# DeltaNet preparation: the block inverse transposed by VectorE in blocks of 32x32, in place of TensorE's products with a unit matrix and ScalarE's copies

## The reference, cut to what matters

```
lower = where(strict, einsum('bhnid,bhnjd->bhnij', k_beta, k) * decay, 0.0)
rhs   = concatenate([v * beta[..., None], k_beta * exp(gc)[..., None]], axis=-1)
sol   = triangular_solve(eye(C) + lower, rhs, left_side=True, lower=True, unit_diagonal=True)
u, w  = sol[..., :dv], sol[..., dv:]
```

## Time and profile before

| | |
|---|---|
| median of 3 runs | 3337.93 us (3333.68 to 3339.06) |
| the profiled execution | 3340.42 us, its span 3338.6 us |
| PE busy over the span | 3035.5 us (91%), 24428 matmul instructions |
| DVE, ACT, POOL busy | 1317.9 us (39%), 1020.9 us (31%), 479.6 us (14%) |
| the preparation, layer 0 | from about 520 to 704 us of the span |
| the preparation, layer 1 | from about 2240 to 2426 us |
| L1372, the turns on PE | 93.3 us busy, 2880 instructions |
| L1214, the turns' copies on ACT | 57.5 us busy, 120 instructions |

### The profile page before, as it was taken

How to read it: one execution, slowest core, us unless ns; L and a number is a source line. 1 busy time by engine, 2 the same in 40 slices (tenths; PEclk the granted TensorE clock), 3 DMA queues, 4 the chain that set the end, 5 groups by cost and what they waited for, 6 DMA issues and landing times. The chain is left out here.

```text
span 3338.6 us, 64798 instructions
## 1 busy us (share of the span) xinstructions
PE 3035.5 (91%) x24428; PEld 1647.8 (49%) x24429; DVE 1317.9 (39%) x2704; ACT 1020.9 (31%) x1799; POOL 479.6 (14%) x534
## 2 busy tenths in 40 slices
PE   6998898979989999999987898989989899988996
PEld 3554676974543333433332554768955333333331
DVE  3433643444533333333326443634445333322234
ACT  2222442322223333333324232442222222222232
POOL 0010004321010000000007010005231100000004
PEclk8998998999999999999999999989989999999998
DMA  9302330013339999899859210410034599999956
GB/s 382 120 8 82 128 123 5 4 68 134 158 132 346 358 356 358 329 390 387 352 223 349 88 41 22 160 42 4 4 144 170 230 407 424 424 424 423 424 216 239
DMA packets 133673, 724.22 MB, mean 217 GB/s; under 512 B 24800, under 2 KB 42720, under 8 KB 96736
## 3 DMA queue, kind: packets, MB, share of 16 engines
q1 hardware_dynamic: 84800, 544.14, 41.8%
q0 software_dynamic: 28224, 102.77, 8.0%
q10 hardware_dynamic: 20448, 74.46, 5.5%
HBM read 619.62 MB, written 101.71 MB: 216 GB/s over the span
## 5 line engine op out<-in xcount | busy, mean ns | idle before, releaser
L2303 PE MATMUL psum<-arena 128*64 x1792 | 822.9, 614 | 61.3 <-DVE arena L2402 61.3
L2305 PE MATMUL psum<-arena 128*64 128x512 f32 x1792 | 824.5, 613 | 0.0
L2303 PEld LDWEIGHTS psum<-arena 128*64 128x64 f32 x1792 | 243.0, 141 | 542.0 <-issue 542.0
L2325 PE MATMUL psum<-arena 128*64 x896 | 408.3, 599 | 10.9 <-DVE arena L2406 10.9
L827 PE MATMUL psum<-arena 128*128 128x480 f32 (+3 forms) x1088 | 403.2, 527 | 15.7 <-PEq L164 8.4
L2327 PE MATMUL psum<-arena 128*64 128x512 f32 x896 | 408.4, 598 | 0.0
L827 PEld LDWEIGHTS psum<-arena 128*128 128x128 f32 x1088 | 207.9, 194 | 189.7 <-issue 177.8
L2273 POOL DMA_INDIRECT arena<-h,arena x112 | 109.4, 977 | 1263.1 <-PE psum L2293 1239.5
L2325 PEld LDWEIGHTS psum<-arena 128*64 128x64 f32 x896 | 123.9, 139 | 257.3 <-issue 257.3
L2410 DVE TENSOR_TENSOR arena<-arena,psum 128x256 f32<-128x256 f32 x112 | 47.2, 422 | 513.9 <-ACT arena L2359 513.8
L2371 ACT COPY arena<-arena 128x2048 f32 x114 | 217.1, 1904 | 91.6 <-DMA arena<-in_w_gu 87.6
(11 more groups left out here) (357 smaller groups left out, 4308.4 us busy)
## 6 DMA issues: line engine op xcount, KB each, us to landing
arena<-in_w_gu SPq DMA_DIRECT2D x130, 2048.0 KB
arena<-in_w_dn SPq DMA_DIRECT2D x130, 1024.0 KB
y_slots<-arena ACTq DMA_DIRECT2D x122, 512.0 KB
arena<-in_ada SPq DMA_DIRECT2D x24, 2048.0 KB
y_slots<-arena SPq DMA_DIRECT2D x4, 4096.0 KB
arena<-in_w_gdn SPq DMA_DIRECT2D x6, 1536.0 KB
arena<-in_w_out SPq DMA_DIRECT2D x2, 4096.0 KB
arena<-in_w_tok SPq DMA_DIRECT2D x4, 1920.0 KB
```

Source lines behind the costliest of these rows:

```text
L2303: nc.tensor.matmul(psum[half(0), 2 + r, :], xT[:, r, rows_of(k, 0)], W[:, bass.ds(at + k * 2 * DE, 2 * DE)], start=(k == 0), stop=(k == DK ...
L2305: last = nc.tensor.matmul(psum[half(1), 2 + r, :], xT[:, r, rows_of(k, 1)], late_gu[:, k * 2 * DE:(k + 1) * 2 * DE], start=(k == 0), stop= ...
L2325: nc.tensor.matmul(psum[half(0), bank, :], hT[r][:, rows_of(j, 0)], W[:, bass.ds(at + GU + c, 512)], start=(j == 0), stop=(j == 1))
```

## The change

The turn is done by DVE: right behind its subtraction of a level it transposes `DT` into `U`, with one instruction for 128x384 that transposes each block of 32x32 in place. Up to level 4 the blocks of the inverse are at most 32 wide, so all that lies outside the diagonal blocks of 32x32 is zero, and the result is the same. PE's `turn_inverse` and ACT's `take_inverse` are gone with the semaphore between them. The turn behind level 0 becomes `first_inverse` on DVE, behind the updates of slot 2. Two waits that the removed code had are put elsewhere: `lower` of level 1 waits for the copy of u that empties its bank, and `solve` waits for the copies of the tile before.

```
@@ scalar @@
-                        def take_inverse(G, v):
-                            for d in range(2):
-                                c = chain(G, d)
-                                act.wait_ge(tr_done[c], nth(G, v) + 1)
-                                nc.scalar.copy(U[:, G, d], psum[:, 4 + c, 0:GW]).then_inc(d_done[c], 1)
...
@@ tensor, in lower @@
                                 pe.wait_ge(d_done[c], nth(G, v - 1) + 1)
+                                if v == 1 and G >= 2:
+                                    pe.wait_ge(u_copied, 2 * (G - 2) + d + 1)
...
-                        def turn_inverse(G, v):
...
-                                        last = nc.tensor.matmul(psum[half(r), 4 + c, b], DT[half(r), G % 3, d, b], cst("unit")[half(r)], start=True, stop=True)
-                                last.then_inc(tr_done[c], 1)
...
                         def solve(G):
                             pe.wait_ge(it_done, 2 * min(G + 3, NT))
+                            if G:
+                                pe.wait_ge(wt_copied, 2 * G)
...
@@ vector @@
+                        def turn_inverse(G, d):
+                            nc.vector.transpose(U[:, G, d], DT[:, G % 3, d]).then_inc(d_done[chain(G, d)], 1)
+
+                        def first_inverse(G):
+                            for d in range(2):
+                                dve.wait_ge(dt1_done, 2 * G + d + 1)
+                                turn_inverse(G, d)
+
                         def update(G, v):
                             for d in range(2):
...
                                 nc.vector.tensor_tensor(DT[:, G % 3, d], DT[:, G % 3, d], psum[:, 4 + c, 0:GW], ALU.subtract).then_inc(dt_done[c], 1)
+                                if v < LAST:
+                                    dve.wait_ge(dt_done[c], nth(G, v - 1) + 1)
+                                    turn_inverse(G, d)
...
                             for T, v in live:
-                                if v == 1:
-                                    dve.wait_ge(dt1_done, 2 * T + 2)
                                 update(T, v)
+                            if a == 2 and G + 1 < NT:
+                                first_inverse(G + 1)
```

More of the change, by code:

```diff
@@ L1164, in phase_gdn_prepare @@
                     S("masked"), S("dt1_done"), S("u_prod"), S("wt_prod"), S("u_copied"), S("wt_copied"))
-                x_prod, x_done, dt_prod, dt_done, tr_done, d_done = [
-                    [S(f"{name}{c}") for c in range(4)] for name in ("x_prod", "x_done", "dt_prod", "dt_done", "tr_done", "d_done")]
+                x_prod, x_done, dt_prod, dt_done, d_done = [
+                    [S(f"{name}{c}") for c in range(4)] for name in ("x_prod", "x_done", "dt_prod", "dt_done", "d_done")]
                 half = lambda r: slice(64 * r, 64 * r + 64)
@@ L1226, in _ @@
                         take_q(0)
-                        take_inverse(0, 0)
                         for G, a, live in slots:
@@ L1233, in _ @@
                                 tail(G - 1)
[L1234 to L1238, removed]
                     @block.gpsimd
@@ L1396, in _ @@
                         turn_q(0)
-                        turn_inverse(0, 0)
                         for G, a, live in slots:
@@ L1411, in _ @@
                                 turn_q(G + 1)
[L1412 to L1416, removed]
                     @block.vector
@@ L1455, in update @@
                                 nc.vector.tensor_tensor(DT[:, G % 3, d], DT[:, G % 3, d], psum[:, 4 + c, 0:GW], ALU.subtract).then_inc(dt_done[c], 1)
+                                if v < LAST:
+                                    dve.wait_ge(dt_done[c], nth(G, v - 1) + 1)
+                                    turn_inverse(G, d)
                         gated(0)
+                        first_inverse(0)
                         for G, a, live in slots:
```

## The result

The changed kernel takes 3274.09 us (median of 4 runs, 3271.93 to 3276.72), the kernel before 3336.1 us (4 runs, 3333.68 to 3339.06): a ratio of 0.9814, interval 0.9802 to 0.9826. Forecast were 3270 us and a range of 3258 to 3311. The profiled executions took 3340.42 and 3274.05 us, 66.4 apart, where the sum said 67.6.

The account below looks back on a forecast made before the run. PE bounds the kernel. Per layer, first tile 4.5, four full tiles 25.9, last tile 2.4 and last levels 0.95 us sum to 33.8, so 67.6 for both: 3270 us from the median, range 3258 to 3311.

Parts of the forecast that it names:

- the sum: Whole program: savings of 33.8 us a layer in the preparation stage, 67.6 us for both layers.
- PE bounds the tile, and 7.24 us come off: Full tile: PE busy for all 27.94 us, so removing the turns leaves 20.70 us if PE never waits.
- The transpose costs 0.56 us: Each 128x384 transpose on DVE, taken from a 558 ns DVE operation of same shape in SBUF only.
- Both bounds, 0.36 and 0.96: Transpose time in us: 0.36 from below, as a copy; 0.96 from above, if a column costs twice.
- Pairs of 1.07 us, DVE's cadence of 0.47: DVE in a full tile: update plus its transpose takes 0.60 + 0.47 us; one update starts every 0.47 us.
- PE waits 0.76 us in slot 1, so 21.46 a tile: Slot 1's lower groups wait 0.02 + 0.37 + 0.37 us for late DVE; full tile 20.70 + 0.76, 6.48 less.
- The cover by `gate_rows`: Start of a tile: first transposes run under PE's gate_rows and cost nothing; uncovered, in the last tile, up to 2.3 us.
- The single loop: One level of a chain with only one tile live: period 3.74 us in place of 4.64.
- The clock: Rival: PE's granted clock stays low through the tiles after its waits; 3306 us, slower if all groups double; chance 0.03.
- quick: Rival: a transpose takes 0.36 us, as a copy, so PE never waits; 38 us a layer, 3262 us; chance 0.10.
- slow: Rival: a transpose takes 0.96 us and DVE bounds; tile 24.5 us, 15.7 a layer, 3307 us; chance 0.13.
- nothing was given back behind the barrier: Rival denied here: the stage shrinks but a later one gives it back, 3338 us; chance 0.03.

Follow-up runs that it names:

- two moves of a few lines: Changed kernel with first transposes ahead of slot 2's updates, and products and gated at the front of slot 0; together 3260.15 us, ratio to before 0.9788.
- `products` first: Changed kernel with the next tile's products ahead of slot 0's lower products on PE, and gated ahead of its masks on VectorE; 3268.49 us.
- halves: Changed kernel with each transpose done as two of 192 columns; 3280.93 us, one run.

## Why the prediction was right, step by step

- **PE bounds the tile, and 7.24 us come off.** Right, and shown by putting the products back.
- **The transpose costs 0.56 us.** 0.571 measured, by the nearest row. Both bounds, 0.36 and 0.96, were far off; the row of the same shape and memory was the one to take. The estimate of 0.58 from the Trainium skill (VectorE: DVE Perf Modes, The three transpose paths) was as good: its 311 ns for 128 columns in bf16 lies close to the fit here, 171 + 1.04 x 128 = 304 ns in float32, an estimate, since no run here transposes 128 columns.
- **Pairs of 1.07 us, DVE's cadence of 0.47.** Measured 1.05 to 1.08. The rule that VectorE starts nothing before its pipeline is empty (the Trainium skill, VectorE: DVE Perf Modes, The DRAIN you can't avoid) does not describe this trace: a transpose of 0.58 us is followed by the next update 0.50 us after its start (608.21 to 608.71). The same section of the Trainium skill adds that an operation that is not held starts earlier, which the prediction left out. The overlap is also why DVE's busy time in a full tile is 16.9 to 17.2 us and not the 18.3 forecast: that sum counted the shared time twice.
- **PE waits 0.76 us in slot 1, so 21.46 a tile.** Measured 0.73 and 21.35 to 21.48. That the waits are DVE's late queue of slot 0 is shown by moving `gated` forward: 20.69.
- **The cover by `gate_rows`.** Right: the first transposes cost nothing in full tiles and 2.08 us in the last.
- **The single loop.** Here the step was wrong, by little. I said 3.74 us; it is 3.94. The timeline of the first tile after the change:

```profile
548.95 1.97 PE L1337 MATMUL psum<-arena 64*64 64x64 f32 x48 [0.96 <-DVE arena L1423]
549.37 0.58 DVE L1423 STREAM_TRANSPOSE arena<-arena 128x384 f32<-128x384 f32 x1
549.91 0.56 DVE L1420 TENSOR_TENSOR arena<-psum,arena 128x384 f32<-128x384 f32 x1
550.75 1.74 PE L1347 MATMUL psum<-arena 64*64 64x64 f32 x48
...
552.25 0.58 DVE L1423 STREAM_TRANSPOSE arena<-arena 128x384 f32<-128x384 f32 x1
...
552.89 1.97 PE L1337 MATMUL psum<-arena 64*64 64x64 f32 x48 [0.39 <-DVE arena L1423]
```

The mask of the first direction is done at 550.47, but its `correct` starts at 550.75. In PE's list `lower` of the second direction stands ahead; that waits for its transpose (549.95) and keeps PE until 550.75. I had put the distance of 1.05 us between the directions into the end of the loop and not into PE's list. By this reading the loop must lose the wait where a pair is short and grow by all of it where it is long. With 32-column transposes the pair is some 0.7 us, and the loop is 3.39 (656.00 to 659.39), just the sum without the wait, 0.96 + 0.61 + 0.96 + 0.60 + 0.21 + 0.05. With two transposes the loop is 4.86 us, where the sum without the wait is 4.24:

```profile
682.05 0.92 PE L1339 MATMUL psum<-arena 64*64 64x64 f32 x24 [1.03 <-DVE arena L1429]
683.57 0.92 PE L1339 MATMUL psum<-arena 64*64 64x64 f32 x24 [0.60 <-DVE arena L1429]
684.31 1.74 PE L1349 MATMUL psum<-arena 64*64 64x64 f32 x48
686.91 0.92 PE L1339 MATMUL psum<-arena 64*64 64x64 f32 x24 [0.86 <-DVE arena L1429]
```

There `correct` starts 2.26 us behind its own `lower` (682.05 to 684.31), right behind the other's. It costs 0.2 us a loop after the change, under 2 us in all: from the first `lower` of the last two levels to the end of the count above it is 8.42 us (661.43 to 669.85) and not 7.95, a gain of 0.5 us a layer and not 0.95. It is also part of what the kernel with two transposes exceeded its forecast by.
- **From the stage to the whole.** The stage moved by 68.9 us against 67.6, and the two profiles by 66.4. The medians differ by 62.0, since the profiled execution of the kernel before lay 4.3 us above its median. The 3.8 us between the forecast from the median (3270.3) and 3274.1 add up as follows: 4.3 for that, 2.6 lost in the rest of the span, less 1.3 more from the stage, less 1.8 by which the median before came out lower with a fourth run. Runs of one kernel spread over 5 us, so none of this speaks for or against a step of the sum.
- **The rivals.** The clock stayed at 1.00 through the full tiles and the last tile. That it did so in the last tile was not assured: behind the wait there it fell to 0.50 for some us in both layers of two other kernels and in one layer of a third; the transpose was neither quick nor slow; nothing was given back behind the barrier, as the rest of the span changed by 2.6 us, which is less than the 8 us by which it differs among the kernels above, all with the same code there.

## What to carry to other kernels

Where one engine is busy without a gap, as PE was here, work taken from it comes off in full, and the price is what the receiving engine's queue then makes it wait: walk one period of both lists with durations from the trace, the handing on included, and the waits show themselves to a tenth of a us. After such a change search the newly late engine's list for work that stands further back than its inputs ask; here two moves of a few lines, one of them shown to be worth nothing before, took another 8.8 us off the stages (the medians, 3274.1 and 3260.2, lie further apart, but the ratio to before went only from 0.9814 to 0.9788). In the walk every instruction ahead in an in-order list counts, that of the sibling chain too.

## What the runs showed of the hardware

- VectorE's transpose in blocks of 32x32, float32, SBUF to SBUF: 571 ns for 128x384, 371 for 128x192 (336 for one right behind another, which overlaps it), 212 for 128x32; 1.04 ns a column behind some 171 ns, so as any two-input operation of that shape and not at the rate of its copy.
- It waits for its input with no more than the usual gap: 0.58 us from the update's start to the transpose's (607.63 to 608.21), and 0.06 us from its end to PE's next product (552.25 + 0.58 to 552.89).
- A group of 24 PE instructions of 64x64 holds PE for 0.70 us in a row of such groups, and for 1.30 us at a granted clock of 0.50 (four of them in 5.18 us, 659.15 to 664.33 with each transpose twice). In layer 1 of the kernel before, groups came some 0.8 us apart for a while at a granted clock of 1.00 (2399.71 to 2402.80, four in 3.09 us), and so did the four `correct` groups at 644.66 to 647.82 with the first transposes ahead; why stays open.
- Behind PE's wait of 1.87 to 3.37 us in front of the last tile, the granted clock fell to 0.50 in five of eight cases: in both layers with each transpose twice (waits of 3.37 and 3.22 us) and with `products` first (2.08 and 2.08), in layer 0 with halves (1.98), and not in layer 1 with halves (1.95) nor in either layer of the changed kernel (2.08 and 1.87). What decides it no run here shows.
